# Seven block products for 18 of 22 gate/up tiles instead of 8, run back to back

## The reference

```
def _swiglu(x, w_gate, w_up, w_down):
    return (jax.nn.silu(x @ w_gate) * (x @ w_up)) @ w_down
```

## Time and profile before

| | |
|---|---|
| median of 3 runs | 2103.65 us (2103.55 to 2104.06) |
| span of the profiled execution | 2102.9 us |
| instructions in it | 31133 |
| PE busy | 2066.9 us, 98% |
| DVE, ACT, POOL busy | 1351.0, 1013.6, 722.4 us |
| eight mixed bodies, first / second / third stage | 169.47 / 169.35 / 169.83 us |

### The profile page before, as it was taken

One profiled execution on the slowest core, in us unless ns is written; L12 is line 12 of the kernel. 1 busy time (PEld: TensorE's weight loads), 2 busy tenths in 40 slices (PEclk: granted clock), 3 DMA queues, 4 the chain that ended last, 5 costly groups with the idle time before them and its releaser, 6 DMA issues.

```text
span 2102.9 us, 31133 instructions
## 1 busy us (share of the span) xinstructions
PE 2066.9 (98%) x10658; PEld 1753.4 (83%) x10658; DVE 1351.0 (64%) x2278; ACT 1013.6 (48%) x1788; POOL 722.4 (34%) x544
## 2 busy tenths in 40 slices
PE   8999999999999999999999999999999999999998
PEld 6778888888988888988887788888878888888886
DVE  6497863667752366674277889899767337676523
ACT  4466663533433353434344577767655325344322
POOL 2133452513233163442337511211165315233331
PEclk9999999999999999999999999999999999999999
DMA  5333263334433244443335322222364534445331
GB/s 175 96 103 103 76 225 100 119 117 155 140 123 97 80 130 130 150 149 110 91 94 171 100 71 89 73 80 86 118 203 131 178 97 126 135 132 167 100 99 61
DMA packets 74383, 251.31 MB, mean 120 GB/s; under 512 B 8264, under 2 KB 8520, under 8 KB 73776
## 3 DMA queue, kind: packets, MB, share of 16 engines
q1 hardware_dynamic: 51120, 182.08, 28.2%
q0 software_dynamic: 11456, 40.72, 5.8%
q10 hardware_dynamic: 11712, 27.27, 3.5%
HBM read 229.57 MB, written 18.89 MB: 118 GB/s over the span
## 4 chain that ended last, share of the span: by engine, by line
PE 87%; DVE 8%; ACT 2%; issue 2%; DMA 1%; DVEq 0%; SPq 0%; ACTq 0%
PE bank L188 25%; PE bank L190 25%; PE bank L189 25%; PE bank L195 3%; PE bank L194 3%; PE bank L2166 1%; DVE w_lo L162 1%; DMA w_raw<-stream 1%; PE bank L2833 1%; PE bank L920 1%; PE bank L2835 1%; PE bank L347 1%; PE bank L349 1%; PE bank L354 1%; PE bank L2841 1%
## 5 line engine op out<-in xcount | busy, mean ns | idle before, releaser
L162 DVE TENSOR_TENSOR w_lo<-w_raw,w_hi 128x1024 fp32r<-128x1024 f32 x337 | 454.0, 1350 | 410.2 <-ACT w_hi L157 407.0
L188 PE MATMUL bank<-xn_hi,w_hi 128*128 128x512 f32 (+1 forms) x1432 | 554.5, 387 | 6.1 <-DVE w_lo L162 4.2
L157 ACT ACTIVATE w_hi<-w_raw 128x1024 fp32r<-128x1024 f32 x337 | 354.7, 1055 | 417.7 <-PE bank L190 249.6
L189 PE MATMUL bank<-xn_lo,w_hi 128*128 128x512 f32 (+1 forms) x1432 | 538.6, 376 | 0.0
L190 PE MATMUL bank<-xn_hi,w_lo 128*128 128x512 f32 (+1 forms) x1432 | 538.5, 376 | 0.0
L188 PEld LDWEIGHTS bank<-xn_hi,w_hi 128*128 128x128 f32 x1432 | 270.2, 189 | 58.0 <-DVE h L622 6.0
L190 PEld LDWEIGHTS bank<-xn_hi,w_lo 128*128 128x128 f32 x1432 | 269.5, 188 | 50.1
L189 PEld LDWEIGHTS bank<-xn_lo,w_hi 128*128 128x128 f32 x1432 | 270.3, 189 | 44.6 <-issue 2.6
L188 PE MATMUL bank<-down_hi,w_hi 128*128 128x512 f32 x528 | 205.8, 390 | 0.0
L190 PE MATMUL bank<-down_hi,w_lo 128*128 128x512 f32 x528 | 205.4, 389 | 0.0
L189 PE MATMUL bank<-down_lo,w_hi 128*128 128x512 f32 x528 | 205.4, 389 | 0.0
(11 more groups left out here) (473 smaller groups left out, 4228.1 us busy)
## 6 DMA issues: line engine op xcount, KB each, us to landing
w_raw<-stream SPq DMA_DIRECT2D x337, 512.0 KB, 3.6
s_raw<-stream POOLq DMA_DIRECT2D x48, 512.0 KB, 6.4
spill_g<-gate_out ACTq DMA_DIRECT2D x16, 256.0 KB, 2.0
m_more<-spill_g POOLq DMA_DIRECT2D x3, 1024.0 KB, 13.2
x<-xt SPq DMA_DIRECT2D x4, 512.0 KB, 6.9
x<-xt ACTq DMA_DIRECT2D x1, 2048.0 KB, 11.5
spill_x<-x ACTq DMA_DIRECT2D x1, 2048.0 KB, 7.6
spill_ga<-ga_out ACTq DMA_DIRECT2D x8, 256.0 KB, 3.3
```

The source lines that it names most:

```text
L157: nc.scalar.activation(w_hi[:, slot, :], w_raw[:, slot % 2, :], ACT.Copy).then_inc(split_hi, 1)
L162: nc.vector.tensor_tensor(w_lo[:, slot, :], w_raw[:, slot % 2, :], w_hi[:, slot, :], ALU.subtract).then_inc(split_lo, 1)
L188: nc.tensor.matmul(to, a_hi, b_hi, start=start, stop=False, skip_group_check=True)
L189: nc.tensor.matmul(to, a_hi, b_lo, start=False, stop=False, skip_group_check=True)
```

## The change

Now 18 of the 22 tiles of a stage are computed by seven products, and four plain tiles run ahead of them. The loop body holds two tiles, q = 0 and q = 1, which use banks 0 to 2 and 4 to 6 (`XZY`). No plain matmuls stand between the products any more: PE runs x, z, x, z, x, y, x, where x, z, y are three banks of the tile, and the product with T4 is now accumulated into bank x as the last one, after DVE has read the bank. So there are three snapshots and three `joined` a tile, and no fourth bank.

Since only sums and the upper half of the up chunk are used, the second `w_hi`/`w_lo` of a tile is made for half a chunk (`UPPER`). Two raw buffers alternate: `s_raw` for q = 0, and for q = 1 the unused quarters of `xn_hi` and `xn_lo` (`s_holes`: pieces of 256 values, 1 KB each; `s_first` once, before these are free). ACT makes the high part of each sum twice: into `s_hi` for PE, and into PSUM bank 3 or 7 (`s_high_twice`), from where DVE takes it for the low part, in place of `s_hi`. Only the first such tile of a stage does without the copy. The high and low parts of a tile's sums are made while PE works on the tile before. POOL's squares in the second stage move to ACT (`Square` into bank 3) and DVE (an addition).

```diff
-            nc.scalar.activation(w_hi[:, slot, :], w_raw[:, slot % 2, :], ACT.Copy).then_inc(split_hi, 1)
-
-        def low_part(dve, ring, slot):
+            nc.scalar.activation(w_hi[:, slot, at], w_raw[:, slot % 2, at], ACT.Copy).then_inc(split_hi, 1)
+
+        def low_part(dve, ring, slot, at=slice(0, CW)):
 
             dve.wait_ge(split_hi, RING * ring + (slot + 1))
-            nc.vector.tensor_tensor(w_lo[:, slot, :], w_raw[:, slot % 2, :], w_hi[:, slot, :],
+            nc.vector.tensor_tensor(w_lo[:, slot, at], w_raw[:, slot % 2, at], w_hi[:, slot, at],
                                     ALU.subtract).then_inc(split_lo, 1)
...
-        FIRST_BODY = 3
-        BODIES = FT // 2 - FIRST_BODY
+        PLAIN = 4
+        SEVENS = FT - PLAIN
+        BODIES = SEVENS // 2
+        UPPER = slice(HT * P, CW)
         C1, C3, C2, C4 = range(4)
         S2, S1, S3, S4 = range(4)
         S_AT = ((0, 0), (1, 1), (1, 0), (0, 1))
+        S_ORDER = (S1, S2, S4, S3)
+        SUM_OF = {S1: 1, S3: 2, S2: 3, S4: 4}
+        XZY = ((0, 1, 2), (4, 5, 6))
+        s_first = sb("s_first", [P, 2, 2, HT * P], F32, A0 + 12 * K)
+        s_holes = [sb(f"s_holes{g}", [P, HT, S], F32, (56 + 16 * g) * K) for g in range(2)]
...
+            def raw_of(n, i, q):
+
+                g, half = S_AT[n]
+                if q == 0 or (isinstance(i, int) and i == 0):
+                    return (s_raw if q == 0 else s_first)[:, g, half, :].rearrange("p (a b) -> p a b", b=H)
+                return s_holes[g][:, 2 * half:2 * half + 2, H:S]
+
+            def part_of(tile, n):
+
+                return tile[:, n, :].rearrange("p (a b) -> p a b", b=H)
+
+            def copy_of(n):
+
+                return banks[(3, 7)[n in (S2, S3)]][:].bitcast(F32R)
+
+            SECOND = (4, 5, 6, 7)
+            AHEADS = (4, 5, 6, 7)
...
+                def seven(i, q):
+                    to_x, to_z, to_y = (banks[n][:, 0:H] for n in XZY[q])
+                    gate = ready(pe, first_in, gate_of(q), i, N_IN)
+                    pe.wait_ge(s["product"], tiles_done(i, q, -1))
                     block(to_x, w_hi[:, gate, a1], w_lo[:, gate, a1], xn_hi[:, lower, left], xn_lo[:, lower, left],
                           stop=False).then_inc(m["scaled"], 1)
+                    pe.wait_ge(c["lo"], part_made("lo", i, q, 1))
+                    block(to_z, s_hi[:, S1], s_lo[:, S1], t_hi[:, C1], t_lo[:, C1], stop=False).then_inc(m["scaled"], 1)
+                    pe.wait_ge(c["lo"], part_made("lo", i, q, 2))
+                    pe.wait_ge(c["gate"], snapped(i, q, 1))
+                    block(to_x, s_hi[:, S2], s_lo[:, S2], t_hi[:, C2], t_lo[:, C2], False, False).then_inc(m["scaled"], 1)
+                    pe.wait_ge(c["lo"], part_made("lo", i, q, 3))
+                    pe.wait_ge(c["gate"], snapped(i, q, 2))
+                    block(to_z, s_hi[:, S4], s_lo[:, S4], xn_hi[:, upper, right], xn_lo[:, upper, right], False
+                          ).then_inc(m["scaled"], 1)
+                    pe.wait_ge(c["lo"], part_made("lo", i, q, 4))
+                    pe.wait_ge(c["gate"], snapped(i, q, 3))
+                    block(to_x, s_hi[:, S3], s_lo[:, S3], t_hi[:, C3], t_lo[:, C3], False, False).then_inc(m["scaled"], 1)
                     block(to_y, w_hi[:, gate, a2], w_lo[:, gate, a2], xn_hi[:, upper, left], xn_lo[:, upper, left]
                           ).then_inc(used, 1)
...
+                    up = ready(pe, first_in, gate_of(q) + 1, i, N_IN)
+                    pe.wait_ge(c["gated"], combined(i, q, 2))
+                    block(to_x, w_hi[:, up, a2], w_lo[:, up, a2], t_hi[:, C4], t_lo[:, C4], False).then_inc(used, 1)
+
+                with pe.Fori(0, BODIES) as i:
+                    for q in range(2):
+                        seven(i, q)
...
+                def s_high_twice(n, i, q):
+                    s_high(n, i, q)
+                    act.wait_ge(c["lo"], part_made("lo", i, q, S_ORDER.index(n) - 1))
+                    nc.scalar.activation(copy_of(n).rearrange("p (a b) -> p a b", b=H), raw_of(n, i, q), ACT.Copy
+                                         ).then_inc(c["hi"], 1)
...
+                def seven(i, q, more):
+                    x_bank, z_bank, _ = XZY[q]
+                    following = (i, 1) if q == 0 else (i + 1, 0)
+                    ahead(high_part, act, first_in, gate_of(q), i, N_IN)
+                    act.wait_ge(c["gated"], combined(i, q, 0))
+                    act.wait_ge(m["scaled"], multiplied(i, q, 1))
+                    snap(0, x_bank)
+                    ahead(high_part, act, first_in, gate_of(q) + 1, i, N_IN, UPPER if more else slice(0, CW))
+                    act.wait_ge(m["scaled"], multiplied(i, q, 2))
+                    snap(1, z_bank)
+                    if more:
+                        if joint and q == 0 and not (isinstance(i, int) and i == 0):
+                            act.wait_ge(f["added"], i)
+                        s_high_twice(S1, *following)
+                    act.wait_ge(m["scaled"], multiplied(i, q, 3))
+                    snap(2, x_bank)
+                    if more:
+                        act.wait_ge(s["product"], tiles_done(i, q))
+                        s_high_twice(S2, *following)
+                        act.wait_ge(m["scaled"], multiplied(i, q, 4))
+                        s_high_twice(S4, *following)
+                        act.wait_ge(m["scaled"], multiplied(i, q, 5))
+                        s_high_twice(S3, *following)
+                    if joint and q == 1 and more:
+                        if isinstance(i, int):
+                            nc.scalar.activation(fin_r[:], x[:, 0, :], ACT.Square).then_inc(f["added"], 1)
+                        else:
+                            act.wait_ge(c["lo"], part_made("lo", *following, 3))
+                            nc.scalar.activation(banks[3][:], x[:, i, :], ACT.Square).then_inc(f["square"], 1)
+                    silu_of(q, 4 * i + (2 * (b + PLAIN + q) + 1))
...
+                def seven(i, q, more):
+                    x_bank, z_bank, y_bank = XZY[q]
+                    following = (i, 1) if q == 0 else (i + 1, 0)
+                    ahead(low_part, dve, first_in, gate_of(q), i, N_IN)
+                    ahead(low_part, dve, first_in, gate_of(q) + 1, i, N_IN, UPPER if more else slice(0, CW))
+                    if more:
+                        s_low(S1, *following, copy_of(S1))
+                    dve.wait_ge(m["scaled"], multiplied(i, q, 4))
+                    dve.wait_ge(c["gate"], snapped(i, q, 3))
+                    joined(silu[q][:, H:S], z_bank, 2)
+                    if more:
+                        s_low(S2, *following, copy_of(S2))
+                    dve.wait_ge(m["scaled"], multiplied(i, q, 5))
+                    joined(h_tile(i, q, 1), x_bank, 1)
+                    if more:
+                        s_low(S4, *following, copy_of(S4))
+                    finished(dve, first_in, gate_of(q), i, N_IN)
+                    joined(silu[q][:, 0:H], y_bank, 0)
+                    dve.wait_ge(c["gated"], combined(i, q, 3))
+                    nc.vector.tensor_tensor(silu[q][:], silu[q][:], norm_r[:], ALU.mult).then_inc(s["scaled"], 1)
+                    nc.vector.tensor_tensor(h_tile(i, q, 1), h_tile(i, q, 1), norm_r[:, H:S], ALU.mult)
+                    if more:
+                        s_low(S3, *following, copy_of(S3))
+                    finished(dve, first_in, gate_of(q) + 1, i, N_IN)
+                    nc.vector.tensor_tensor(h_tile(i, q, 0), banks[x_bank][:, 0:H], norm_r[:, 0:H], ALU.mult
+                                            ).then_inc(s["scaled"], 1)
+                    gated(h_tile(i, q), q, 4 * i + (2 * (b + PLAIN + q) + 2), 2 * i + (b + PLAIN + q + 1))
+                    if joint and q == 1 and not isinstance(i, int):
+                        dve.wait_ge(f["square"], i)
+                        dve.wait_ge(f["added"], i)
+                        nc.vector.tensor_tensor(fin_r[:], banks[3][:], fin_r[:], ALU.add).then_inc(f["added"], 1)
...
+                def raw_to(i, q):
                     for g in range(2):
-                        pool.dma_start(s_raw[:, g].rearrange("p h w -> p (h w)"), stream[first + g]).then_inc(gates_in[g], 16)
-
-                def sums(i):
-                    for g in range(2):
-                        pool.wait_ge(gates_in[g], 16 * i + (gates_loaded[g] + 16 * (1 - FIRST_BODY)))
-                    a11, a12, a21, a22 = (s_raw[:, g, half, :] for g in range(2) for half in range(2))
+                        chunk = stream[4 * i + (first_in + gate_of(q) + g)]
+                        if q == 0 or (isinstance(i, int) and i == 0):
+                            to = (s_raw if q == 0 else s_first)[:, g].rearrange("p h w -> p (h w)")
+                            pool.dma_start(to, chunk).then_inc(gates_in[q], 16)
+                        else:
```

(39 more changed lines are left out.)

215 lines of the change are left out of this document (63 added, 152 removed).

## The result

The changed kernel took 2192.47 us (median of 4 runs, 2192.21 to 2194.81), the kernel before 2103.86 in the same series. The ratio is 1.0425 (95% interval 1.041 to 1.044): 88.6 us slower. The prediction said 2181 with a range of 2128 to 2206.

The account below looks back on a forecast made before the run. A loop of waits through POOL, ACT and DVE (11.7 us a tile against PE's 10.1) was taken as the bound. A stage's 18 tiles take 216 us against 191.4; three stages 74, plus 3.6: +77, 2181 us, range 2128 to 2206.

Parts of the forecast that it names:

- Pitch and PE's floor: PE: 256-column matmuls start 0.120 us apart, 512-column ones 0.228; a seven-product tile takes 10.1 us, a plain one 10.9.
- The ring of 11.7: Seven-product tiles: POOL's wait, loads and four sums, ACT's copies and DVE's low parts form a loop of 11.7 us a tile.
- Where PE waits: At a tile's fifth product for the third snapshot and seventh for the second join, 1.6 us a tile together.
- The blocking: DVE and POOL shut each other out on two-SBUF-operand operations: 0.65 us in the loop, bounds 0 and 1.7.
- Sums of work: Work per seven-product tile: DVE 7.0 us, ACT about 7.7, POOL 6.5, all below PE's 10.1.
- Start of a stage: First seven-product tile: the fourth product comes late by 6.4 us, bounds 2 and 9.
- End of a stage: Before the down products: silu, high part and low part leave PE idle 2.7 us, bounds 2.4 and 3.5.
- Second stage's squares: Squares leave POOL and cost DVE 0.6 us on every second tile: 3.6 us.
- Late pieces of 1 KB: Rival, 10%: loads into the holes land in 13.2 us, every second tile takes one us more: 2205.
- The ring without blocking: Rival, 15%: weight low parts fall into POOL's issue time; 29 us less, and 13 less at the starts: 2139.
- Faster: Rival, 11%: the loop closes in under 10.1 us and PE sets the pace, 22 us less: 2082.

Follow-up runs that it names:

- e8: After with ScalarE issuing the raw loads, six plain tiles ahead, and the first two down high parts made before the last Silu: 2100.6 us, 0.9983 of the kernel before.
- e12: e8 with the last square of the second stage added one tile earlier: 2096.5 us, ratio 0.996 to the kernel before.
- e1: After with GpSimd's wait and loads of tile T+2 placed behind the first of the four sums of tile T+1: 2143.9 us, ratio 1.0192.
- e5: After with ScalarE, not GpSimd, issuing both raw loads of tile T+2, behind its second snapshot: 2139.5 us, ratio 1.0164.
- e9: After with VectorE's low part of the fourth sum (S3) moved ahead of the two products with the norm: 2206.3 us, ratio 1.0488.
- e6: After with the weight chunk's high and low parts made ahead of the four sums' parts in the last plain tile: 2184.8 us, ratio 1.0379.
- e7: After with six plain tiles instead of four, the first sums' parts spread over the fourth and fifth: 2161.4 us, ratio 1.0269.
- e4: After with ScalarE's first two high parts of `h` for the down products made ahead of the last Silu: 2183.6 us, ratio 1.0376.
- after: The changed kernel itself, against the kernel before: 2192.47 us, ratio 1.0425.
- e10: e8 with the loads issued behind the third snapshot and the second stage's last square added one tile earlier: 2117.7 us, ratio 1.0065 to the kernel before.
- e2: After with GpSimd's wait and loads of tile T+2 placed behind the second of the four sums of tile T+1: 2145.1 us, ratio 1.0193.

## Why the prediction was right, step by step

- **Pitch and PE's floor.** Right: where nothing is late, tiles take 10.07 or 10.08 us (the first tiles of e8 and e12).
- **The ring of 11.7.** Right, and shown: e1 takes one sum out and the first stage's tiles fall to 10.43, e5 takes GpSimd's wait out and 53 us go. Step by step, from the tile above: low part's end to issue 0.66 (0.66 predicted); to the first sum 1.56 (1.3; this is the hole buffer, put at 1.45); the four sums 5.63 (5.25 and 0.65 for blocking); ACT 1.15 (1.2); DVE 2.71 (2.7). The next tile, with the other buffer, has 0.71, 1.16, 6.01, 1.15 and 2.71: more blocking, less issue, 11.74 again. The tiles behind the first took 186.0, 190.2 and 187.3 us, 563.4 in all; predicted were 16 x 11.7 - 0.7 for each stage and 3.6 for the squares, 563.1.
- **Where PE waits.** Right, in place and size. The waits that the profile lists, 35.8 us for snapshots (13 of them at the starts) and 34.0 for the second join, are only 1.2 us a tile, since a matmul's modelled length covers part of a gap. By distances of starts, as the prediction reads a pitch, the fifth product of the tile above comes 537.56 - 536.73 - 0.12 = 0.71 late and the seventh 541.36 - 540.42 - 0.12 = 0.82, and the matmul behind each a further 0.10 and 0.07. That is 1.70, all that this tile takes over 10.08 (11.78). In the mean of the first stage's 16 tiles it is 0.66 and 0.89, together 1.55, where 1.6 was said.
- **The blocking.** In the ring the size was right: 5.63 and 6.01 us for the four sums, 5.82 in the mean, against 5.9. Off the ring the picture was too mild. I had VectorE's weight low parts at up to 1.9 us, stopped by one sum. In the tile above the pair took 4.26: the first 1.22, the second some 3.0, through two sums. It did no harm there because the pair has room until the join; in e9 it happened to the gating product, and took the whole gain. The Trainium skill, SBUF — State Buffer, "SBUF: two separate sides", has whoever starts first hold the ports for one instruction; here the one that waits is passed over by the next instruction as well (3.94 us in e9).
- **Sums of work.** ScalarE's terms add up to 7.1 us a tile and not 7.7, and the four sums of 1.30 with their gaps to 5.3 and not 5.25. Neither moves the forecast.
- **Start of a stage: the term that was mis-sized.** Predicted +6.4; measured 19.05 - 10.08 = 9.0, 8.7 and 9.2, so 7.7 us too little in all. The wait was right as a whole. PE's rows in the first tile of stage one, and the chain's last link on ACT:

```profile
421.77 0.38 PE L188 MATMUL bank<-t_hi,s_hi 128*128 128x256 f32 x1 [1.77 <-DVE s_lo L678]
429.45 0.58 PE L188 MATMUL bank<-xn_hi,s_hi 128*128 128x256 f32 x1 [4.56 <-ACT snaps L559]
```

```profile
428.50 0.63 ACT L157 ACTIVATE w_hi<-w_raw 128x512 fp32r<-128x512 f32 x1 [5.50 <-DMA w_raw<-stream]
```

  1.77 + 4.56 = 6.3, and the fourth product comes late by the chain that I gave (e6 shortens it, e7 removes it). The first part, spent at the second product on the low parts of the first sums, I had not named; it falls inside the same lateness. What I left out is the clock: behind the idle time the 24 matmuls from 429.45 on take 5.03 us where 24 x 0.12 = 2.88 would do, nearly all of them 0.21 apart, the pace of the lower of the two levels (1.2 GHz). That is 2.15 us in this stage, and the granted clock of the tile is 0.82; it is 0.82 in the first tiles of the other two as well.
- **End of a stage.** Right: 12.64 - 10.08 = 2.56 (2.7 predicted), by the chain named (e4).
- **Second stage's squares.** About right: 4.2 us more than stage one in the tiles (3.6). The third stage, without squares, took 1.3 more too, which I can't explain.
- **The rest.** The sum of the terms as measured is 77 + 7.7 - 0.4 = 84, and the stages up to their down products are 85 longer. The span grew by 87.6. The remainder is in the down products, and mostly the clock again: the first and the third take 121.20 and 123.12 us with a granted clock of 0.99 each, before 119.68 and 121.38. (The 0.94 of the last window is mostly the end of the run, where the kernel before has a low clock too.)
- **Rivals.** Late pieces of 1 KB: did not happen, the holes' loads land in 4.7 us (median) and POOL never waited for them in after. The ring without blocking: no, the sums took 5.63 and 6.01 and not 5.25. Faster: only when the ring, the start and the end are all mended (e12), and still 0.3 to 0.4 us a tile over PE's pace.

## What to carry to other kernels

Sum the way round before the work of each engine. With every engine but TensorE under 70% busy, the order "wait for the last result, load, then sum" set the tile, and moving that one wait took back 49 of the 89 us. When a step on such a ring is made shorter or a load is moved, look at what the released engine then runs into: in e9 that took the whole gain, in e10 more than it. Read waits from distances of starts, and look at the clock behind them: e9 waits no longer a tile than after does, but in longer pieces, and loses 14 us at the slower pace of the matmuls. Here a second copy, so that VectorE reads one operand from PSUM beside a working GpSimd, was worth 12 us in two kernels.

## What was new about the hardware

- VectorE's product of two SBUF operands took 3.94 us beside GpSimd's sums, not 0.69: it waited through two of them in a row (e9).
- With one operand in PSUM the same engine keeps 0.68 us beside a working GpSimd (64 low parts, mean 683 ns), and a weight low part from SBUF that began in GpSimd's issue of a DMA took 1.22 us, the 1.21 of the earlier trace rows, where GpSimd was idle:

```profile
533.59 1.22 DVE L162 TENSOR_TENSOR w_lo<-w_raw,w_hi 128x1024 fp32r<-128x1024 f32 x1
```

  That an issue can hold VectorE up too is not excluded by e9's product, which began in one and would have been over before the first sum.
- ScalarE's copy of 128x512 takes 0.58 us into PSUM and 0.63 into SBUF; the starts are 0.53 apart in both cases, so that back to back nothing is gained.
- Behind a wait of 4.6 us, with one of 1.8 us ahead of it in the same tile, TensorE's matmuls of 256 columns start 0.21 us apart in place of 0.12, and the granted clock of the tile is 0.82. With waits of 0.6 us, twice a tile, the tiles of after kept 1.00; with one wait of up to 2.7 us a tile those of e9 had 0.96 to 0.98.
- A short wait costs TensorE more than the gap that the profile lists: 0.56 listed were 0.71 by distances of starts, and the next matmul came 0.10 late as well.
- The weight chunks landed in 3.6 us (median) before and 3.7 after, but in the second stage in 4.4 after and 5.1 in e2.
